# A mixing convolution partly on TensorE with its sums in PSUM, a later start of a LayerNorm's bookkeeping, and other first loads

## The reference, cut to what matters

```python
def conv_module(a, g, conv_w, conv_b, conv_norm):      # 512 channels, 31 taps, causal
    u = a * jax.nn.sigmoid(g)
    y = lax.conv_general_dilated(u, conv_w[:, None, :], window_strides=(1,), padding=[(30, 0)],
                                 dimension_numbers=("NWC", "WIO", "NWC"), feature_group_count=512)
    return jax.nn.silu(rms_norm(y + conv_b, conv_norm))
...
a, g, q, k, v = jnp.split(rms_norm(x, mix_norm) @ w_in, splits, axis=-1)
x = x + jnp.concatenate([conv_module(a, g, ...), diff_attention(q, k, v, ...)], axis=-1) @ w_out
```

## Time and profile before

| what | us |
|---|---|
| median of 3 runs | 1975.85 (1974.34 to 1976.68) |
| the profiled execution: its time | 1975.4 |
| its span, first to last instruction | 1973.6 |
| TensorE busy | 1809.5 (92%) |
| VectorE busy | 1164.3 (59%) |
| ScalarE busy | 846.7 (43%) |
| GpSimd busy | 337.0 (17%) |
| mean granted TensorE clock | 0.946 of full speed |

### The profile page before, as it was taken

One profiled execution on the slowest core, in us unless ns is written; L12 is line 12 of the kernel. 1 busy time (PEld: TensorE's weight loads), 2 busy tenths in 40 slices (PEclk: granted clock), 3 DMA queues, 4 the chain that ended last, 5 costly groups with the idle time before them and its releaser, 6 DMA issues.

```text
span 1973.6 us, 29577 instructions
## 1 busy us (share of the span) xinstructions
PE 1809.5 (92%) x12095; PEld 1657.4 (84%) x12101; DVE 1164.3 (59%) x1479; ACT 846.7 (43%) x1076; POOL 337.0 (17%) x223
## 2 busy tenths in 40 slices
PE   4987999799999799989999868999999998689999
PEld 3955899699998699979998866999899988669998
DVE  2565655677667665565445894544454558955444
ACT  2343444354455344454435335433443453355332
POOL 6001000258032210000000563000000005630000
PEclk8989999899999999999999977999999998779999
DMA  9501555355510475535554421555555544214552
GB/s 223 171 22 64 195 189 192 117 171 171 188 49 22 144 218 183 190 128 192 191 181 139 150 86 64 167 179 186 170 183 180 190 149 150 86 64 163 179 189 107
DMA packets 211759, 295.22 MB, mean 150 GB/s; under 512 B 6874, under 2 KB 184480, under 8 KB 211552
## 3 DMA queue, kind: packets, MB, share of 16 engines
q1 hardware_dynamic: 207792, 285.62, 43.7%
q0 software_dynamic: 3456, 7.71, 2.0%
q10 hardware_dynamic: 432, 0.79, 0.1%
HBM read 293.04 MB, written 1.05 MB: 149 GB/s over the span
## 4 chain that ended last, share of the span: by engine, by line
PE 77%; DVE 16%; ACT 3%; DMA 2%; issue 1%; SPq 0%; POOL 0%; DVEq 0%; ACTq 0%
PE pg L1670 45%; PE acc L1670 24%; DVE arena L1547 8%; DMA w_raw<-in_attn_w_in 2%; PE acc L2013 1%; DVE op_lo L1132 1%; DVE op_hi L1131 1%; ACT w_hi L727 1%; PE acc L1929 1%; PE pg L1997 1%; PE pg L1999 1%; DVE stats L1168 1%; PE pg L1905 1%; DVE X L1165 1%; PE pg L1734 0%
## 5 line engine op out<-in xcount | busy, mean ns | idle before, releaser
L1670 PE MATMUL pg<-op_hi,w_hi 128*128 128x256 f32 x2536 | 731.7, 289 | 56.1 <-DVE op_lo L1132 23.8
L1114 DVE TENSOR_TENSOR w_lo<-w_raw,w_hi 128x2048 fp32r<-128x2048 f32 x231 | 528.7, 2291 | 405.9 <-ACT w_hi L727 405.9
L1670 PE MATMUL pg<-op_hi,w_lo 128*128 128x256 f32 x2536 | 725.5, 286 | 0.0
L1670 PE MATMUL pg<-op_lo,w_hi 128*128 128x256 f32 x2536 | 725.0, 286 | 0.0
L727 ACT CAST w_hi<-w_raw 128x2048 fp32r<-128x2048 f32 x270 | 514.1, 1904 | 233.1 <-PE pg L1670 151.3
L1670 PEld LDWEIGHTS pg<-op_hi,w_hi 128*128 128x128 f32 x2536 | 494.9, 195 | 65.3 <-issue 22.5
L1670 PEld LDWEIGHTS pg<-op_hi,w_lo 128*128 128x128 f32 x2536 | 495.3, 195 | 3.5 <-issue 0.7
L1670 PEld LDWEIGHTS pg<-op_lo,w_hi 128*128 128x128 f32 x2536 | 494.7, 195 | 0.0
L1670 PE MATMUL acc<-w_hi,op_hi 128*128 128x512 f32 x768 | 301.3, 392 | 1.3 <-DVE op_lo L1377 0.9
L1670 PE MATMUL acc<-w_lo,op_hi 128*128 128x512 f32 x768 | 300.4, 391 | 0.0
L1670 PE MATMUL acc<-w_hi,op_lo 128*128 128x512 f32 x768 | 299.3, 390 | 0.0
(11 more groups left out here) (263 smaller groups left out, 1569.1 us busy)
## 6 DMA issues: line engine op xcount, KB each, us to landing
w_raw<-in_mlp_w SPq DMA_DIRECT2D x64, 1024.0 KB, 5.2
w_raw<-in_ffn_w_gate SPq DMA_DIRECT2D x44, 1024.0 KB, 5.2
w_raw<-in_ffn_w_up SPq DMA_DIRECT2D x44, 1024.0 KB, 5.2
w_raw<-in_ffn_w_down SPq DMA_DIRECT2D x44, 1024.0 KB, 4.7
w_raw<-in_ssm_w_in SPq DMA_DIRECT2D x24, 1024.0 KB, 5.4
w_raw<-in_w_in SPq DMA_DIRECT2D x20, 1024.0 KB, 5.0
w_raw<-in_attn_w_in SPq DMA_DIRECT2D x9, 1024.0 KB, 5.5
w_raw<-in_ssm_w_out SPq DMA_DIRECT2D x8, 1024.0 KB, 4.8
```

Source lines behind the costliest of these rows:

```text
L1114: dve.tensor_tensor(w_lo[:, s, :], w_raw[:, s, :], w_hi[:, s, :].bitcast(F32), ALU.subtract) \
L1670: ins = pe.matmul(psum, l, r, start=first and i == 0, stop=last and i == 2)
```

## The change

- The convolution's four chunks are shared out anew. Chunks 0 to 2 stay on VectorE, all 31 taps, but accumulate in PSUM (`conv_bank`, banks 2 and 3 of `acc`), the last tap writing to `cacc`. Chunk 3 goes to TensorE: for each tap, ScalarE writes a 128x128 matrix with the tap's weights on its diagonal (`diag_tap`, 31 activations in three lots, at n = 1, 3 and 9), and TensorE multiplies it with the shifted `uu`, in fp32, 256 columns, four taps in each attention step, accumulating in `pg` bank 3. GpSimd's ten taps are gone; its splits are no longer interrupted.
- VectorE's instructions per point are now 24, 10, 10, 10, 10, 18, and in the attention 2, 2, 2, 2, 1, 1, 1: 93 in place of 114. The sum of chunk 3 is read behind step 7 (`convolve_last`) and the square of the convolution moves from s = 7 to s = 9.
- The banks that this takes cost double buffering: the heads' sums and spreads have one bank each (new waits on `qk_std` and `qk_ready`), and so do the transposes of the mixed maps.
- The attention starts on the first two heads once their q and k and the v in the way are ready.
- `settle` waits for the end of the turn (`xt_ready`) and not for `xn`; before the SSM projections it is moved behind GpSimd's splits and the last convolution of that stage.
- The first loads: constants come in two parts, 640 KB behind unit 1 and 512 KB behind unit 2. The bias table comes in two DMAs of 448 KB (64 x 8 rows of 219 values), issued once unit 1 has landed, and TensorE flips from overlapping windows of it, two 256-column matmuls for each head.

```diff
-TAPS = [14,11,7,7,7,7,2,2,0,0]
-POOL_TAPS = 10
+TAPS = [24, 10, 10, 10, 10, 18, 2, 2, 2, 2, 1, 1, 1]
+PE_TAPS = 4
+DIAGS = [0, 10, 20, CK]
...
+        def conv_bank(c):
+            return acc[:, 2 + c // 2, (c % 2) * T:(c % 2) * T + T]
...
@@ sync
-                    sp.dma_start(att_c, A["consts"][:, P:P + n_att]).then_inc(const_in, 16)
+                    sp.dma_start(att_c[:, 0:n_rope], A["consts"][:, P:P + n_rope]).then_inc(const_in, 16)
+                if n == 2:
+
+                    sp.dma_start(att_c[:, n_rope:n_att], A["consts"][:, P + n_rope:P + n_att]).then_inc(const_in, 16)
...
@@ gpsimd
-            for h in range(BH):
-                for qt in range(TT):
-                    for r in range(2):
...
+            pool.wait_ge(raw_ready[1], 16)
+            for r in range(2):
+                src = bass.AP(rpb.tensor, rpb.offset + (NA_KH - 3 - r) * RPB_C + NA_KW - 1 - (GRID_W - 1),
+                              [[1, 64], [RPB_R * RPB_C, BH], [1, NA_W]])
+                pool.dma_start(na_raw[r * 64:r * 64 + 64, :, :], src).then_inc(bias_in, 16)
...
-                pool.wait_ge(norm_ready, NORM_AT[name] + 1 + KC // 2)
+                pool.wait_ge(xt_ready, TURN_BANK[name] + KC // 2)
...
+            for n in range(2, 17):
+                split(U_SSM + n)
+            pool.wait_ge(conv_done, len(SSM_COLS) - 1 - Z_UNITS)
             settle(1, "ln2_0")
             rows_load(2)
-            for n in range(2, 17):
-                split(U_SSM + n)
...
@@ scalar
+                def diag_taps(j):
+                    for k in range(DIAGS[j], DIAGS[j + 1]):
+                        wc = COL["conv_w"] + l * P + 4 * k + 3
+                        ins = act.activation(diag_tap(k), ident[:, :], ACT.Identity, scale=pcol[:, wc:wc + 1])
+                    ins.then_inc(diag_ready, 1)
...
@@ vector
-                            ins = dve.scalar_tensor_tensor(out=cacc[:, c, :], in0=uu[:, c, k:k + T], scalar=w,
-                                                           in1=cacc[:, c, :], op0=ALU.mult, op1=ALU.add)
+                            ins = dve.scalar_tensor_tensor(out=conv_bank(c) if k < CK - 1 else cacc[:, c, :],
+                                                           in0=uu[:, c, k:k + T], scalar=w,
+                                                           in1=conv_bank(c), op0=ALU.mult, op1=ALU.add)
...
+                def convolve_last():
+
+                    dve.wait_ge(pe_conv, l + 1)
+                    link.all_but(0)
+                    bc = COL["conv_b"] + 4 * l + 3
+                    dve.tensor_scalar(cacc[:, 3, :], pg[:, 3, 0:T], pcol[:, bc:bc + 1], None, ALU.add).then_inc(cconv, 1)
...
@@ tensor
+                if i:
+
+                    pe.wait_ge(qk_std, i)
...
+                if i:
+
+                    pe.wait_ge(qk_ready, i)
...
-                pe.wait_ge(qk_ready, 4 * l + 4)
-                pe.wait_ge(v_ready, 2 * l + 2)
...
+                        if s < 2:
+                            pe.wait_ge(v_ready, 2 * l + s + 1)
+                        if s % DH == 0:
+                            pe.wait_ge(qk_ready, 4 * l + 2 * (s // DH) + 2)
...
+                    if s < 2 * DH:
+
+                        for k in range(PE_TAPS * s, min(PE_TAPS * (s + 1), CK)):
+                            if k in DIAGS:
+                                pe.wait_ge(diag_ready, 3 * l + DIAGS.index(k) + 1)
+                            ins = pe.matmul(pg[:, 3, 0:T], diag_tap(k), uu[:, 3, k:k + T], start=k == 0,
+                                            stop=k == CK - 1)
```

More of the change, by code:

```diff
@@ L61 @@
 MIX_COLS = [2 * U, 0, 3 * U, U] + [2 * CCH + i * U for i in (0, 2, 1, 3, 4, 5)]
-TAPS = [14,11,7,7,7,7,2,2,0,0]
-POOL_TAPS = 10
-assert 2 * sum(TAPS) + POOL_TAPS == 4 * CK
+TAPS = [24, 10, 10, 10, 10, 18, 2, 2, 2, 2, 1, 1, 1]
+PE_TAPS = 4
+DIAGS = [0, 10, 20, CK]
+assert sum(TAPS) == 3 * CK
 U_ATT = 0
@@ L181 @@
 N_SUMS = 4 + 3 * DEPTH
-CONST_BLK = 48
+CONST_ROPE, CONST_ATT, CONST_SSM, CONST_BLK = 16, 32, 48, 64
+NA_ROWS = 6
+NA_W = (NA_ROWS - 1) * RPB_C + GRID_W
 N_PAR = 20
@@ L323, in two_blocks, with diag_tap @@
         cacc = cv(4, T)
-        pool_acc, pool_tap = (v.rearrange("p a n -> p (a n)") for v in (lam_q, lam_k))
+        def diag_tap(k):
+            home = (xn[:, 0, :], O2.rearrange("p h t -> p (h t)"), osq.rearrange("p c t -> p (c t)"), xn[:, 1, :])[k // 8]
+            return home[:, (k % 8) * P:(k % 8) * P + P]
+        def conv_bank(c):
+            return acc[:, 2 + c // 2, (c % 2) * T:(c % 2) * T + T]
         sq = turn_buf[:, :, :, :].rearrange("p a b t -> p a (b t)")
@@ L699, in _ @@
             for l in range(DEPTH):
[L700 to L712, removed]
+                for u in range(U_MIX[l] + 2, U_MIX_OUT[l] + OUT_UNITS):
                     split(u)
@@ L1020, in _ @@
                         split(u + 2)
+                    if n in (1, 3):
+                        diag_taps(n // 2)
                     bank = pg[:, n % 4, :]
@@ L1043, in _ @@
                             act.wait_ge(qk_spread, i - 1)
-                        act.activation(hdev[:, i % 2, :], acc[:, i % 2, 0:8], ACT.Sqrt, bias=lnb[:, 1:2],
+                        act.activation(hdev[:, i % 2, :], acc[:, 0, 0:8], ACT.Sqrt, bias=lnb[:, 1:2],
                                        scale=1.0 / HD).then_inc(qk_std, 1)
@@ L1075, in _ @@
                         act.wait_ge(csum, l + 1)
-                        act.activation(cdev, acc[:, 2, 0:TT], ACT.Sqrt, bias=lnb[:, 1:2],
+                        act.activation(cdev, pg[:, 0, 0:TT], ACT.Sqrt, bias=lnb[:, 1:2],
                                        scale=1.0 / CCH).then_inc(cstd, 1)
@@ L1524, in gated_columns @@
                     dve.wait_ge(u_ready, 4 * l + n + 1)
-                count = [CK, CK, CK, CK - POOL_TAPS]
-                taps = [(k, c) for k in range(TAPS[0]) for c in (0, 1)]
-                left = [[(k, c) for k in range(TAPS[0] if c < 2 else 0, count[c])] for c in range(4)]
+                taps = [(k, c) for k in range(TAPS[0] // 2) for c in (0, 1)]
+                left = [[(k, c) for k in range(TAPS[0] // 2 if c < 2 else 0, CK)] for c in range(3)]
                 taps += [tap for _, tap in sorted(((j + 0.5) / len(some), tap) for some in left
@@ L1536, in convolve_on @@
                 def convolve_on(i):
-                    for k, c in taps[done[0]:done[0] + 2 * TAPS[i]]:
+                    for k, c in taps[done[0]:done[0] + TAPS[i]]:
                         wc = COL["conv_w"] + l * P + 4 * k + c
@@ L1566, in head_norm @@
                     dst = head_pair(n)
-                    dve.tensor_tensor(dst, dst, acc[:, 2 + i % 2, :], ALU.mult).then_inc(qk_ready, 1)
+                    dve.tensor_tensor(dst, dst, acc[:, 1, :], ALU.mult).then_inc(qk_ready, 1)
                 gated_columns(1)
@@ L1876, in _ @@
                             pe.wait_ge(bias_ready, h - 1)
-                        pe.matmul(acc[:, h % 2, :], att_const("na_flip"),
-                                  na_bias[:, h, :, :].rearrange("p a n -> p (a n)"), start=True, stop=True) \
-                            .then_inc(bias_flipped, 1)
+                        for qt in range(TT):
+                            ins = pe.matmul(acc[:, h % 2, qt * T:(qt + 1) * T].rearrange("p (a k) -> p a k", k=GRID_W),
+                                            att_const("na_flip"), na_rows(h, qt), start=True, stop=True)
+                        ins.then_inc(bias_flipped, 1)
                 if n == 8:
```

66 lines of the change are left out of this document (36 added, 30 removed).

## The result

The changed kernel takes 1887.59 us (median of four runs, 1886.61 to 1891.65) and the kernel before 1975.09 in the same comparison: a ratio of 0.956, with a 95% interval of 0.9544 to 0.9577, or 87.5 us. The forecast was 1899.0, 76.9 us less than before. The profiled execution has a span of 1884.5 us (before 1973.6, so 89.1 less) at a mean granted clock of 0.980 (before 0.946).

A forecast was written before the change was run, and what follows sets the result against it. TensorE, busy 92% of the span, bounds the kernel; gains lie where it waits or runs at the lower clock. Mixing stages 36.4, LayerNorms 17.5 and start 23 sum to 76.9 us less: 1899.0 us, 8 in 10 for 1877 to 1926.

The forecast's parts named there:

- The stage until the first score: Mixing stage up to VectorE's first take of a score: taps at 0.40 us in PSUM, TensorE pacing, 22.6 us earlier.
- ScalarE's diagonals: Mixing stage: 31 diagonals at up to 0.38 us each; the eleven at n = 9 delay 0 to 4, counted as nothing.
- The attention: Mixing stage after the first score: products fit the phase's 39.1 us at full clock, 0.4 us added a layer.
- the stall with its half clock: Attention, about step 4: a split holds a short VectorE instruction, half clock follows; 4 us a layer, bounds 0 to 19.
- The LayerNorms: Turns without settle beside VectorE: 4.5, 8.5 and 4.5 us earlier, together 17.5, range 8 to 26.
- The start: First loads: table behind unit 1, TensorE begins unit 2 at about 25, not 48.32; 23 us, range 14 to 25.
- Half clock through both attentions: Rival: TensorE at half clock in both attentions, 2 x 15 us back, 1929 us, chance 0.14.
- load-bound: Rival: rows and table still crowd unit 2 at the start, only 9 us kept there, 1913 us, chance 0.10.
- All goes well: Rival: full clock through both attentions (8 us) and settle never ahead of VectorE's instructions (8 us): 1883 us, chance 0.15.
- Taps in PSUM at 1.1 us: Slower rival: each PSUM tap waits for the previous write; from 1.1 us all gains go, 1991 at 1.2, chance 0.04.

The follow-up runs named there:

- the later split: The changed kernel with GpSimd's split of the third output unit waiting for the convolution's last rounded output: 1873.58 us.
- the mixing part alone: The kernel before with only the mixing stage changed: 1931.91 us, 43.4 less.
- the second profile of before: The unchanged kernel before, profiled once more: 1976.43 us, span 1974.6.
- the part alone: The kernel before with one part changed: under LayerNorms, settle's later wait and move, 1955.32 us; under the start, the new first loads, 1951.62 us.
- the later settle: The changed kernel with the first and third LayerNorm's settle started only when the MLP's third hidden group is ready: 1880.79 us.
- the pair without the hold: The later split with all 31 diagonal products, 1873.58 us, and the same kernel with 29 of them left out, 1872.58 us.

## Why the prediction was right

**The stage until the first score** was the strongest step. Taps at 0.40 were taken, 0.409 measured (18 in 7.36 us; other lots 0.40 to 0.42), beside splits too; no stall at the seventh projection; TensorE sets the pace with 5.86, 0.89 and 0.79 for unit, spread and sums where the prediction had 5.8, 1.10 and 0.95. The first take came 66.6 us into the stage; 68 was forecast, and 90.4 it was. That is 23.8 earlier against 22.6; most of the difference is the overstated sums and spreads. The surcharge for a PSUM source by the Trainium skill ("VectorE: DVE Perf Modes", "The TRN2 errata — SBUF-src ops pay a fixed extra latency per instruction"), an estimated 0.065 us a tap, doesn't appear: 0.409 against 0.393 in SBUF.

**ScalarE's diagonals** took 3.4 us for the eleven at n = 9 (1.28 and 2.14), within the bound of 0.38 each.

**The attention** is where the sum was off, by two terms that partly cancel. I let the phase's 39.1 us stay and added 0.4 for the products; with them and without a hold the phase is 34.7 (the later split), so this term was 4.8 us too high. The half clock at which the 39.1 had been measured doesn't account for it, since a phase at half clock without a hold takes 33.2. The old phase had holds of its own in it, beside GpSimd's taps and beside the split that follows them:

```profile
1182.19 0.22 DVE L1601 TENSOR_SCALAR arena<-arena 128x2 f32<-128x2 f32 x1
...
1193.80 3.17 DVE L1601 TENSOR_SCALAR arena<-arena 128x2 f32<-128x2 f32 x1
...
1192.44 4.51 POOL L621 TENSOR_TENSOR w_lo<-w_raw,w_hi 128x2048 fp32r<-128x2048 f32 x1
```

This one instruction beside a split is 3.0 us too long, and four L1605 beside GpSimd's taps take 0.39 to 0.82 us where others take 0.17, some 4.6 us in all. And I put 4 us for the stall with its half clock; the later split shows 7.0 a layer by the medians, 5.9 and 7.2 by the traces. The mechanism was named rightly (a split that holds a short instruction, a stall, half clock behind it); TensorE's stall, 3.67 us, came at step 4's transposes as forecast, though the held instruction (`n2`, the negated maximum that the exponential needs) is that of the second step. In sum the phase is 40.6 long where the forecast had 43.5. This and the earlier first take make 22.3 and 20.9 us for the two layers, 43.4 by the mixing part alone, against 36.4: 7 of the 10.6 us by which the forecast missed.

**The LayerNorms**: 4.5, 8.5 and 4.5 were forecast; 5.6, 7.1 and 4.5 are in the traces (6.8, 7.4 and 5.0 against the second profile of before), 20.0 by the part alone. That a turn without the hold is worth 8.5, and settle gives part of it back on the splits and `h`, is what the later settle shows: 8.5 us at the first LayerNorm, or 9.7 by the second profile of before, so the agreement to a tenth is luck. Why the second LayerNorm gave 1.1 to 1.4 less than 8.5 with settle gone from there, no run shows.

**The start**: 23 was forecast, 24.4 at unit 3 and 23.7 by the part alone. Unit 2 was forecast at 25, and came at 24.16. The reason was right but not divided: about 15 to 18 us are the form of the table, with the split constants and fewer bytes, and 7 to 9 its place, with all that GpSimd loads behind it.

**The rivals.** Half clock through both attentions didn't come: the clock was at 0.50 only behind the stall (0.50 and 0.65 from 1114 to 1122) and in the tail, and the pair without the hold shows that it is then the products that keep it at 1.00. What all 31 products would cost at half clock, which the rival put at 15 us a layer, no run shows. The start wasn't load-bound. *All goes well*, at 1883, was nearer to the result than the forecast in time, yet not in kind: both of its conditions were unmet, and once they were met the time was 1866 to 1872. Taps in PSUM at 1.1 us were never near; that rival's time at 1.2 us comes out by its own terms at 1993, not 1991.

## What to carry to other kernels

Where VectorE and GpSimd work side by side, look for every VectorE instruction with two SBUF inputs, and for small ones on the path of a handover, beneath a long GpSimd instruction: put an operand in PSUM, or put the GpSimd work where VectorE has slack. Idle pieces of TensorE between handovers could here be filled with 12.5 us of work for 0.5 to 1.5 us, and the filling kept the clock of all that lies around it. When a forecast takes over a phase's length from the old trace, look for the held instructions in it: here they were some 4.6 of 39.1 us.

## What the runs showed of the hardware

- A `TENSOR_SCALAR` of 128x2 in SBUF, with one SBUF input, was held 4.45 us beside a GpSimd split and takes 0.17 alone. The Trainium skill ("SBUF — State Buffer", "Who interferes with whom") counts `tensor_scalar` among those that can take the shared ports; this row agrees. Two reductions in SBUF that ran within a split in the kernel before (1193.27 and 1193.48, the split from 1192.44 to 1196.95) weren't held: 0.29 and 0.41 us, as elsewhere.
- The length of a half-clock phase at one and the same place differed by 4.8 us between two executions of one kernel (62.1 and 66.9 us for the first attention), while their totals differed by 1 us (1975.4 and 1976.43). A stage's difference between two single profiles is known to about 5 us here, unless it is seen in several.
- While GpSimd issued its loads at the start, behind two DMAs of the table in rows of 219 values (GpSimd busy 4.45 to 5.00 of 5.00 us), the DMA engines were as busy but moved 0.7 of the rate: 279 and 257 GB/s with the table first, 287 and 264 with it later, in place of 380 and 369.
